# Memory norm and key/value tiles of a cross-attention moved from attention's head into the two stages before it

## The reference, cut to what matters

```
def rmsnorm(x, g):
    y = xf * lax.rsqrt(jnp.mean(xf * xf, axis=-1, keepdims=True) + EPS)
    return (y * g.astype(F32)).astype(x.dtype)

h = h + concatenate([y_a, y_b, y_c, y_d]) @ w_out            # mixing stage
h = h + cross_attention(rmsnorm(h, xa_norm), rmsnorm(mem, xa_mem_norm), xa_wq, xa_wkv, xa_wo)

def cross_attention(hn, mn, wq, wkv, wo):
    q = (hn @ wq)                          # 4 heads of 256
    k, v = jnp.split(mn @ wkv, 2, axis=-1) # 256 x 1024 each
    p = softmax(q . k * XA_HD ** -0.5);  o = p . v
    return o @ wo
```

## Time and profile before

| | us |
|---|---|
| median of 3 runs | 3453.59 (3451.35 to 3454.88) |
| profiled execution | 3451.87 |
| its span | 3449.8 |
| TensorE busy | 3108.7 (90%) |
| VectorE busy | 2188.5 (63%) |
| ScalarE busy | 1305.1 (38%) |

### The profile page before, as it was taken

How to read it: one execution, slowest core, us unless ns; L and a number is a source line. 1 busy time by engine, 2 the same in 40 slices (tenths; PEclk the granted TensorE clock), 3 DMA queues, 4 the chain that set the end, 5 groups by cost and what they waited for, 6 DMA issues and landing times. The chain is left out here.

```text
span 3449.8 us, 52263 instructions
## 1 busy us (share of the span) xinstructions
PE 3108.7 (90%) x20768; PEld 2541.8 (74%) x20768; DVE 2188.5 (63%) x3324; ACT 1305.1 (38%) x2088; POOL 493.1 (14%) x650
## 2 busy tenths in 40 slices
PE   5989889679999849988999959999899999899998
PEld 4767667478888628875888847888778887778776
DVE  4656566567765667614444447777777776677776
ACT  3636454445553122112333333333343333343443
POOL 2323333266771001100000000000000000000000
PEclk9999999889999969999999979999999999999999
DMA  3252525512220034342111123333332323767764
GB/s 126 76 183 73 182 67 165 177 58 76 70 64 18 1 140 159 134 143 96 49 61 67 55 110 110 111 110 116 125 120 104 116 104 128 232 188 231 232 205 145
DMA packets 195260, 407.64 MB, mean 118 GB/s; under 512 B 14576, under 2 KB 98800, under 8 KB 188656
## 3 DMA queue, kind: packets, MB, share of 16 engines
q1 hardware_dynamic: 195056, 404.79, 35.7%
HBM read 287.27 MB, written 117.46 MB: 117 GB/s over the span
## 5 line engine op out<-in xcount | busy, mean ns | idle before, releaser
L2632 PE MATMUL ffn_ps<-ffn_t_p,ffn_w_p 128*128 128x512 f32 x3696 | 847.3, 392 | 44.1 <-DVE ffn_w_p L2808 27.4
L2632 PEld LDWEIGHTS ffn_ps<-ffn_t_p,ffn_w_p 128*128 128x128 f32 x3696 | 698.5, 189 | 192.9 <-DVE ffn_w_p L2808 29.5
L2647 PE MATMUL ffn_ps<-ffn_t_p 128*128 128x512 f32 x2112 | 490.5, 394 | 25.1 <-DVE ffn_t_p L2954 18.8
L2647 PEld LDWEIGHTS ffn_ps<-ffn_t_p 128*128 128x128 f32 x2112 | 398.2, 190 | 117.4 <-DVE ffn_t_p L2954 26.4
L410 PE MATMUL proj<-hn_high,w_high 128*128 128x512 f32 x672 | 281.1, 418 | 36.4 <-POOL w_low L330 36.4
L330 POOL TENSOR_TENSOR w_low<-w_ring,w_high 128x1024 fp32r<-128x1024 f32 x84 | 207.9, 2480 | 444.5 <-ACT w_high L441 444.5
L410 PE MATMUL proj<-hn_high,w_low 128*128 128x512 f32 x672 | 266.8, 397 | 0.0
L410 PE MATMUL proj<-hn_low,w_high 128*128 128x512 f32 x672 | 266.7, 397 | 0.0
L2658 ACT ACTIVATE ffn_w_p<-ffn_w_p_sums 128x512 fp32r<-128x512 f32 x176 | 111.1, 631 | 378.4 <-DVE ffn_w_p_sums L2829 378.2
L2954 DVE TENSOR_TENSOR ffn_t_p<-ffn_ring,ffn_t_p 128x1536 fp32r<-128x1536 f32 x88 | 154.7, 1758 | 131.2 <-ACT ffn_t_p L2728 130.9
L2728 ACT ACTIVATE ffn_t_p<-ffn_ring 128x1536 fp32r<-128x1536 f32 x88 | 130.9, 1488 | 266.8 <-DVE ffn_ring L2950 263.1
(11 more groups left out here) (460 smaller groups left out, 5849.1 us busy)
## 6 DMA issues: line engine op xcount, KB each, us to landing
ffn_ring<-in_w_up SPq DMA_DIRECT2D x44, 1024.0 KB, 5.6
ffn_ring<-in_w_down SPq DMA_DIRECT2D x88, 512.0 KB, 5.4
w_ring<-in_w_feat SPq DMA_DIRECT2D x84, 512.0 KB, 3.6
ffn_ring<-scratch_values SPq DMA_DIRECT2D x88, 257.0 KB, 4.5
scratch_gates<-ffn_gate SPq DMA_DIRECT2D x44, 512.0 KB, 2.6
ffn_ring<-scratch_gates SPq DMA_DIRECT2D x88, 256.0 KB, 3.8
feats<-scratch_scan SPq DMA_DIRECT2D x16, 896.0 KB, 4.5
scratch_values<-ffn_raw SPq DMA_DIRECT2D x22, 513.0 KB, 3.5
```

Source lines behind the costliest of these rows:

```text
L2632: mm = pe.matmul(bank(name, s), w_part(name, a)[:, k * P:(k + 1) * P], t_part(name, b)[:, k * TB:(k + 1) * TB], start=k == a == b == 0, st ...
L2647: mm = pe.matmul(ps[:, DOWN_BANKS[2 * t + c]], down_part(n, x)[:, HID + t * TC:HID + (t + 1) * TC], down_part(n, y)[:, c * DH:(c + 1) * DH ...
```

## The change

The memory norm and eleven of the sixteen key/value tiles leave `attend_memory`. SBUF at its top keeps three buffers (`memory_buffers`) from `state_space` on: the normed memory `mn`, a ring of now six slots, and `kv`.

In `state_space` SyncE loads the memory and tiles 0 to 5 once all y are done; the memory lies where the states were. ScalarE squares it behind the last GELU, takes the root, and does the scaling, which VectorE did; VectorE does the two tiny steps behind its copies into `yt`. TensorE transposes behind the gate products, into banks 4 to 7; ScalarE applies the gain, four columns of tiles after each of the first two roots. Tiles 0 to 4 follow on TensorE behind the column sums. SyncE issues the loads of tiles 6 and 7 ahead of the stores of blocks 2 and 3.

In `mix_out` TensorE computes tile 5 ahead of `fin1`, tile 6 between `fin1` and `fin2`, tiles 7 to 10 behind `fin2`, in two buffers of PSUM; ScalarE evicts tiles 5 to 8 between its four weight pieces and tiles 9 and 10 ahead of `high(0, 0)`. SyncE loads tiles 8 to 10 between the output weight and x, and then, each when a slot is free, tiles 11 to 15 and the first of `wq_t`; before the stage ends it waits for them.

`attend_memory` begins with tile 11.

```diff
+MEM_KEPT = 3 * KT * N_MEM * 4 + 6 * D_MODEL * 4
+KV_IN_S5, KV_IN_MIX, KV_RING = 5, 6, 6
+
+
+def memory_buffers(nc):
+
...
+    for name, shape in (("mn", [P, KT, N_MEM]), ("ring", [P, KV_RING, D_MODEL]), ("kv", [P, 2 * KT, N_MEM])):
+        M[name] = nc.alloc_sbuf_tensor_at("mem_" + name, shape, F32, offset=top)
+        top += 4 * int(np.prod(shape[1:]))
+    return M
+
+
+def key_or_value(pe, M, n, out, loaded):
+
+    pe.wait_ge(*loaded)
+    for k in range(KT):
+        mm = pe.matmul(out, M["ring"][:, n % KV_RING, k * P:(k + 1) * P], M["mn"][:, k], start=k == 0, stop=k == KT - 1)
+    return mm
...
+        MT = N_MEM // P
+        flat = h[:].rearrange("p g n -> p (g n)")
+        m_t = flat[:, 0:MT * D_MODEL].rearrange("p (j n) -> p j n", j=MT)
+        m_junk = flat[:, MT * D_MODEL:(MT + 1) * D_MODEL]
+        m_sq = mi[:, 0, 0:MT]
...
+            sp.wait_ge(*y_done.at(0))
+            sp.wait_ge(*l_out.at(0))
+            sp.dma_start(m_t, D["mem"].rearrange("(j p) n -> p j n", p=P)).then_inc(m_in.sem, 16)
+            for n in range(KV_RING):
+                load_kv(n)
             for b in range(NB):
                 sp.wait_ge(*yc_ready.at(0, b))
+                if b >= 2:
+                    sp.wait_ge(*kv_done.at(0, b - 2))
+                    load_kv(KV_RING + b - 2)
                 for t in range(G2):
                     sp.dma_start(D["late"][b * CB:(b + 1) * CB, :, len(LATE) - 1, t].rearrange("c p n -> p c n"),
                                  yt[:, t, b * TB:(b + 1) * TB].rearrange("p (c n) -> p c n", c=CB)).then_inc(stored.sem, 16)
             sp.wait_ge(*stored.at(0))
+            for n in range(KV_RING):
+                sp.wait_ge(*kv_in[n].at(0, int(n < 2)))
...
+            act.wait_ge(*m_in.at(0))
+            for j in range(MT):
+                act.activation(m_junk, m_t[:, j], ACT.Square, accum_out=m_sq[:, j:j + 1]).then_inc(own_a, 1)
+                act.wait_ge(own_a, j + 1)
+            act.sem_inc(m_squared.sem, 1)
+            act.wait_ge(*m_ms.at(0))
+            act.activation(m_sq, m_sq, ACT.Sqrt).then_inc(m_root.sem, 1)
+            act.wait_ge(*m_inv.at(0))
+            for j in range(MT):
+                last = act.activation(m_t[:, j], m_t[:, j], ACT.Copy, scale=m_sq[:, j:j + 1])
+            last.then_inc(m_scaled.sem, 1)
...
+                if b < 2:
+                    for k in range(4 * b, 4 * b + 4):
+                        act.wait_ge(*m_turned.at(0, k // 2))
+                        act.activation(M["mn"][:, k], ps[:, 4 + k // 2, k % 2 * N_MEM:(k % 2 + 1) * N_MEM], ACT.Copy,
+                                       scale=col("xa_mem_norm", k)).then_inc(mn_ready.sem, 1)
+            for n in range(KV_IN_S5):
+                act.wait_ge(*kv_done.at(0, n))
+                act.activation(M["kv"][:, n], ps[:, 4 + n % 4, 0:N_MEM], ACT.Copy).then_inc(kv_out.sem, 1)
...
+            dve.wait_ge(*m_squared.at(0))
+            ts(m_sq, m_sq, 1.0 / D_MODEL, EPS, MUL, ADD).then_inc(m_ms.sem, 1)
+            dve.wait_ge(*m_root.at(0))
+            dve.reciprocal(m_sq, m_sq).then_inc(m_inv.sem, 1)
...
+            pe.wait_ge(*m_scaled.at(0))
+            for k in range(KT):
+                pe.wait_ge(*glu_out.at(0, 4 + k // 2))
+                for j in range(MT):
+                    at = k % 2 * N_MEM + j * P
+                    mm = pe.transpose(ps[:, 4 + k // 2, at:at + P], m_t[:, j, k * P:(k + 1) * P], ident)
+                if k % 2:
+                    mm.then_inc(m_turned.sem, 1)
...
+            pe.wait_ge(*mn_ready.at(0))
+            for n in range(KV_IN_S5):
+                if n >= 4:
+                    pe.wait_ge(*kv_out.at(0, n - 4))
+                key_or_value(pe, M, n, ps[:, 4 + n % 4, 0:N_MEM], kv_in[n % KV_RING].at(0, 0)).then_inc(kv_done.sem, 1)
...
@@ mix_out @@
+                for n in range(KV_RING + 2, KV1):
+                    load_kv(n)
                 for p in range(2):
                     load_x(p, p)
+                for n in range(KV1, KV1 + KV_RING):
+                    sp.wait_ge(*kv_done.at(0, n - KV_RING - KV0))
+                    load_kv(n)
+
+            def load_kv(n):
+
+                src = D["wkv"][n] if n < 2 * KT else D["wq_t"][n - 2 * KT]
+                sp.dma_start(M["ring"][:, n % KV_RING], src).then_inc(kv_in[n % KV_RING].sem, 16)
...
+            for n in range(KV1, KV1 + KV_RING):
+                sp.wait_ge(kv_in[n % KV_RING].sem, 16 * (1 + (KV_RING + 2 <= n - KV_RING < KV1)))
...
+            def kv(n):
+                at = n - KV0
+                if at >= 2:
+                    pe.wait_ge(*kv_out.at(0, at - 2))
+                ready = (kv_in[n % KV_RING].sem, 16 if n >= KV_RING + 2 else 0)
+                key_or_value(pe, M, n, ps_kv[:, at % 2, 0], ready).then_inc(kv_done.sem, 1)
+
             def first():
+                kv(KV0)
                 fin1(0, 0)
+                kv(KV0 + 1)
                 fin2(0)
+                for n in range(KV0 + 2, KV1):
+                    kv(n)
                 fin1(1, 1)
...
+            def keep_kv(n):
+                act.wait_ge(*kv_done.at(0, n))
+                act.activation(M["kv"][:, KV0 + n], ps_kv[:, n % 2, 0], ACT.Copy).then_inc(kv_out.sem, 1)
+
             def first():
                 fin_sq(0, 0, 0)
                 cent_sq(0, 0)
...
                     at = slice(j * PK, (j + 1) * PK)
                     act.wait_ge(*w_in[j].at(0))
                     act.activation(w[0][:, at], w_raw[:, at], ACT.Copy).then_inc(w_high.sem, 1)
+                    keep_kv(j)
                 fin_sq(1, 1, 0)
+                for n in range(PIECES, KV_IN_MIX):
+                    keep_kv(n)
                 high(0, 0)
...
@@ attend_memory @@
                 def _(sp):
-                    sp.dma_start(m_t[:], D["mem"].rearrange("(j p) n -> p j n", p=P)).then_inc(m_in.sem, 16)
-                    for n in range(NT):
-                        if n >= NW:
-                            sp.wait_ge(*multiplied(n - NW))
-                        if n < KVT:
-                            src = D["wkv"][n]
-                        elif n < KVT + KT:
+                    for n in range(KV0 + NW, NT):
+                        sp.wait_ge(*multiplied(n - NW))
+                        if n < KVT + KT:
                             src = D["wq_t"][n - KVT]
...
+                    for n in range(KV0, KVT):
+                        act.wait_ge(*kv_done.at(0, n - KV0))
...
-                    dve.wait_ge(*m_sumsq.at(0))
...
-                    for k in range(KT):
-                        dve.wait_ge(*m_turned.at(0, k))
-                        dve.tensor_scalar(mn[:, k], ps[:, k, 0:N_MEM], col("xa_mem_norm", k), None, ALU.mult)\
-                           .then_inc(mn_ready.sem, 1)
...
-                    pe.wait_ge(*m_scaled.at(0))
-                    for k in range(KT):
...
-                    pe.wait_ge(*mn_ready.at(0))
-                    for n in range(KVT):
-                        pe.wait_ge(*w_in[n % NW].at(0, n // NW))
-                        if n >= 4:
-                            pe.wait_ge(*kv_out.at(0, n - 4))
+                    for n in range(KV0, KVT):
+                        if n >= KV0 + 4:
+                            pe.wait_ge(*kv_out.at(0, n - 4 - KV0))
                         for k in range(KT):
-                            mm = pe.matmul(ps[:, n % 4, 0:N_MEM], ring[:, n % NW, k * P:(k + 1) * P], mn[:, k], start=k == 0,
-                                           stop=k == KT - 1)
+                            mm = pe.matmul(ps[:, n % 4, 0:N_MEM], ring[:, n % NW, k * P:(k + 1) * P], M["mn"][:, k],
+                                           start=k == 0, stop=k == KT - 1)
                         mm.then_inc(kv_done.sem, 1)
```

More of the change, by code:

```diff
@@ L1487, in state_space @@
         coef = sb("coef", [P, 2, NG, 2])
-        w_in = sb("s5_w_in", [P, NG, P])
-        taps = sb("taps", [P, NG, P])
-        step = [sb(f"step{u}", [P, NG, P]) for u in range(2)]
         u_g = sb("u_g", [P, NG, NS])
@@ L1497, in state_space @@
         inv = sb("s5_inv", [P, SEQ])
+        DEAD_BEFORE_KEPT = nc.sbuf_base
+        w_in = sb("s5_w_in", [P, NG, P])
+        taps = sb("taps", [P, NG, P])
+        step = [sb(f"step{u}", [P, NG, P]) for u in range(2)]
+        assert DEAD_BEFORE_KEPT <= M["base"] and nc.sbuf_base <= M["base"] + 4 * (KT * N_MEM + KV_RING * D_MODEL)
+        MT = N_MEM // P
[3 more added lines that the diff above has]
+        m_sq = mi[:, 0, 0:MT]
         ps = mem.enter_context(nc.psum_tensor("s5_ps", [P, NBANK, TB], F32))
@@ L1730, in mix_out @@
         h1_stored = sig("h1_stored", 1, 16)
+        kv_in = [sig(f"m_kv_in{u}", 2, 16) for u in range(KV_RING)]
+        kv_done, kv_out = sig("m_kv_done", KV_IN_MIX), sig("m_kv_out", KV_IN_MIX)
         own_fin, own_pool, sp_hold = (sig("m_own_" + n).sem for n in ("fin", "pool", "hold"))
@@ L1948, in _, with attend_memory @@
             residual(NCH - 1, (NCH - 1) % 2, NCH // 2 - 1)
-def attend_memory(nc, ctx, D, C):
```

(12 more changed lines are left out.)

70 lines of the change are left out of this document (35 added, 35 removed).

## The result

The median is 3407.54 us (3407.37 to 3410.66, 4 runs) against 3452.47 (3448.94 to 3454.88, 4 runs) before: a ratio of 0.9873, 95% interval 0.9856 to 0.989, 44.9 us less. The forecast was 3409.0 and 44.6 less. The profiled execution took 3407.56 us, its span is 3405.5. The page's part 1 after, against the earlier trace rows: TensorE's busy time has hardly moved, its share of the span has risen.

The account below looks back on a forecast made before the run. TensorE fills nine tenths of the span, so time is won only where it waits or runs at half clock. Attention's head -50.1, tail +0.5, mixing head +5.0 sum to -44.6 us: median 3453.59 to 3409.0 us, range 3402 to 3417.

Parts of the forecast that it names:

- Attention's head: Start of attention to the key weights' first product: 69.77 us become 19.6 without norm and eleven tiles, -50.1 us.
- State space tail: End of the state space stage, taking the norm and five tiles: +0.5 us, from -1.0 of clock and +1.5 of stores.
- The halved gap: Tail: transposes shrink TensorE's idle time from 4.02 to 2.1 us, so half clock may not follow; -1.0, between -1.7 and 0.
- The load in front of the last stores: Tail: 512 KB queued before the last pair of stores plus 0.45 us of issue, +1.5 us; bounds 0.45 and 3.9.
- Mixing head: Mixing stage's start to its first product, with six tiles inserted: +5.0 us; bounds +2 and +15.
- tile 8 wait for its load: Mixing head: tile 8's load, queued behind the output weight's four pieces, lands at 1261.4; tiles 9 and 10 follow without gap.
- one more drop in tiles 7 to 9: Mixing head: half clock returning once behind idle gaps of 3.8 and 1.0 us, +0.8 us.
- The first products: Mixing loop's start: half clock for 3.3 us is in the old time already, so nothing was changed there.
- The clock rival: Rival in the mixing head: tiles 8 to 10 at half clock, 6.94 us each, +10.4, total 3419 us; chance 0.12.
- The table load: Tail, ScalarE: 1.28 us ahead of the first sigmoid, which starts some 2 us late and catches up; costs nothing.
- the eight scalings between the roots: Tail, ScalarE: 0.38 us each into mn, delaying the second root by 1.5 us; costs nothing.
- SyncE held in the head until tile 10: Mixing head: SyncE issues loads of tiles 11 to 16; chunk 2's loads queued behind come at 1275 anyway; costs nothing.

Follow-up runs that it names:

- the first two experiments: Changed kernel with all sixteen tiles given back to attention, only the memory norm moved: 3435.7 us; and with only the mixing stage's six tiles given back: 3422.26 us.
- norm alone: Changed kernel with only the memory norm moved, all sixteen tiles in attention's head and tiles 0 to 5 loaded ahead: 3435.7 us, ratio 0.9955.
- chunk ahead: Changed kernel with the split of chunk 0 (mix_high) on ScalarE ahead of the evictions of tiles 9 and 10: 3403.68 us, ratio 0.9861.
- loads behind: Changed kernel with the loads of tiles 6 and 7 issued behind the stores of blocks 2 and 3 instead of ahead: 3411.73 us, ratio 0.9888.
- The two experiments on the loads: Changed kernel with the loads of tiles 6 and 7 behind the stores of blocks 2 and 3: 3411.73 us; or ahead of those of blocks 1 and 2: 3403.7 us.
- tile 5 evicted first: Changed kernel with tile 5 evicted on ScalarE ahead of the first weight piece, so tile 7 need not wait for it: 3404.33 us, ratio 0.9862.
- loads a block earlier: Changed kernel with the loads of tiles 6 and 7 issued ahead of the stores of blocks 1 and 2: 3403.7 us, ratio 0.9867.

## Why the prediction was right, point by point

**Attention's head**, -50.1 forecast, -50.2 measured (19.57 us for 19.6), with each part: 17.4 of tiles, 1.7 of half clock, 0.47 of wait for the last eviction. The norm's chain and the tiles are bare there, which the first two experiments show one by one: 57.48 with sixteen tiles, 40.76 with eleven, 19.57 with five, 13.17 with three. Part of it is luck: that half clock falls on this stretch for just 1.7 us was taken from other stretches, and in the table it is 1.5 with the norm alone, 1.7 in the changed kernel and 2.8 in the execution with the chunk ahead (20.68).

**State space tail**, +0.5 forecast, +2.5 measured: the step that was mis-sized, in both its terms. The halved gap was to give back 1.0 us of clock and gave nothing (36.80 us up to the first reciprocal, 36.77 before). Behind the same gap of 2.27 us the column sums ran at full clock in two of the seven experiments (7.11 us, and 35.11 us up to the first reciprocal: norm alone, loads behind) and took 8.80 us in the other five. So the full bound of -1.7 is real, but less frequent than I took it. The load in front of the last stores cost 2.5 where I took 1.5: 0.45 for the issue, and 2.0 later landing (4.8 us instead of 2.8), more than the 1.25 us of its data. The two experiments on the loads show that this one load is all of it: with nothing in front of the last stores it is 23.24 us from the first reciprocal to the next stage, before 23.15.
The Trainium skill (DMA: Bandwidth & Descriptors, section "Queues, rings and completion order") has each DMA engine take a ring's descriptors in order, and by that rule the stores had to queue. The trace agrees: the slowest store took 4.8 us behind the load and 3.1 with the load issued behind the stores.

**Mixing head**, +5.0 forecast, +5.5 in the head and -1.0 in the loop measured. The order of events is the one foretold: mix_high behind tile 10's eviction, VectorE idle before mix_low, tile 7 behind the eviction of tile 5 (1259.12, idle 3.25 us). I had tile 8 wait for its load, 19.6 us behind the stage's start, and then three tiles. In the three executions that lay this load bare it arrived at 19.9, 20.0 and 20.5 us (tile 5 evicted first, loads a block earlier, chunk ahead). In the changed kernel itself it was not the bound: tile 7, at half clock nearly all its length, ended later, and tile 8 started some 21.0 us behind the stage's start (by its eviction at 1269.38). Against the execution in which the load was the bound and tile 7 ran at full clock that is 1.0 us of head, for which the sum had +0.8 as one more drop in tiles 7 to 9. So the size is right, but the last thing that tile 8 waited for was TensorE, by the clock, and not the load. The first products, which I left at half clock, ran at full clock; in the loop it is 1.0 us less: 200.05 to 200.14 us in the changed kernel and three of the experiments, 200.91 to 201.86 in the four executions whose loop had half clock at its start.

**The clock rival** (tiles 8 to 10 at half clock, +10.4) did not come: their evictions stand 3.45 us apart, a tile at full clock, and the 0.82 over the 17 us is tile 7's, which took 6.5 us. It stands behind the gap of 3.25 us; behind the same gap it took 5.24 us with the chunk ahead and 3.72 with the loads a block earlier. So tile 7's share, some 3 us, is luck of the execution too.
The Trainium skill (TensorE: Matmul & The Clock Gate, section "HAM oscillation — how this bites in real kernels") warns of gaps between bursts. That holds here in its direction: the execution with the 5.68 us gap lost 2.1 us on the tiles behind it, where my expectation had no loss; one execution does not prove the rule. For the shorter gaps the trace shows no fixed outcome: behind equal gaps of 2.27 us, and behind equal gaps of 3.25 us, half clock came in some executions and not in others.

**What hid.** The table load, the eight scalings between the roots, the tiny steps on VectorE behind its copies, SyncE held in the head until tile 10: none shows in a stretch, as forecast. Between the profiled executions it is 44.3 us for the 44.6 forecast, closer than the terms deserve: 2.0 too little in the tail and 0.3 more ahead of it stood against 0.5 too much in head and loop, 0.1 in attention and 1.4 us less in the rest of the kernel. There the change touches only the loads of the weights into the ring; the key and value weights take 27.89 and 27.63 us in both kernels.

What stays open: why the load costs the stores 2.0 us and not 1.25, what decides in which executions half clock comes behind the gates and under tile 7, and why the median with the loads behind the stores is above the changed kernel's.

## What to carry to other kernels

Work that depends only on inputs belongs where the engine that does it is idle, and its price there is not its length but what it pushes: here five tiles behind VectorE's chain cost nothing (seven ended after it, and the stage 1.7 us later), six among ScalarE's and SyncE's work cost 0.7 us each, and in the stage where they stood bare they cost 3.5. Look at every queue into which the moved step is inserted, DMA issues too: a single load in front of a stage's last stores cost more than all moved matrix products in that stage. When several queues wait for one another, move both sides at once; freeing one alone gave 1.6 us of the 5.9 that it won locally.

## What the runs showed of the hardware

TensorE's clock behind a gap is not fixed by the length of the gap alone. Behind the same 2.27 us the same sixteen column sums took 8.80 us in six executions of the changed code and 7.11 in two; behind the same 3.25 us the same tile took 6.5, 5.24 and 3.72 us. Behind a gap of 5.68 us the tiles 8 to 10 took 12.74 us instead of 10.60, some 4.3 us of it at 1.2 GHz; in the changed kernel, where they follow tile 7 without a gap, they ran at 2.4 GHz. The head with the longer gap was 1.0 us longer, though tile 8 started 1.1 us earlier in it, in the one execution seen. And one load of 512 KB took 2.0 us from a store of 256 KB issued right behind it (4.8 us to landing instead of 2.8; 4.7 in the experiment where the loads stood in front of earlier stores).
